# Inverse square roots by exponential and logarithm instead of square root and reciprocal, in a fused six-layer transformer kernel

## The reference

```python
# first stack, 4 layers: mixers diff, moba, swa, diff
for i in range(4):
    h = h + mixer_i(rms_norm(h, attn_norm_g[i]))
    h = h + square(relu(rms_norm(h, mlp_norm_g[i]) @ w_up[i])) @ w_down[i]
h = rms_norm(h, final_norm_g)

# second stack, 2 layers
def layer(x):
    proj = rms_norm(x, norm_g) @ w_in            # 3104 columns, cut into ten parts
    y_conv = pointwise(silu(layer_norm(conv31(a * sigmoid(a_glu))))) * silu(z_conv)
    y_mla  = attention(rms_norm(c_q) @ w_uq, rms_norm(c_kv) @ w_ukv, ...) * silu(z_mla)
    y_sg   = (sg_w @ layer_norm(gelu(v)) + sg_b) * gelu(u) * silu(z_sg)
    return x + concat(rms_norm(y_conv), rms_norm(y_mla), rms_norm(y_sg)) @ w_out

def rms_norm(x, g): return x * rsqrt(mean(x * x) + 1e-6) * g
```

## Time and profile before

| | |
|---|---|
| median of three runs | 1731.67 us (1728.75 to 1737.34) |
| profiled execution | 1732.1 us, span 1730.4 us |
| TensorE busy | 1560.4 us, 90% of the span |
| VectorE busy | 961.6 us, 56% |
| ScalarE busy | 802.0 us, 46% |
| GpSimd busy | 165.6 us, 10% |
| mean granted clock of TensorE | 0.947 of full speed |

### The profile page before, as it was taken

The page is one execution under the profiler, slowest core; times in us unless marked ns, Lnnn a source line. Parts: engine busy times, 40 slices in busy tenths (PEclk is TensorE's granted clock), DMA queues, the critical chain, the costliest instruction groups (busy, mean ns, idle before and its releaser), DMA issues. The chain is left out here.

```text
span 1730.4 us, 21899 instructions
## 1 busy us (share of the span) xinstructions
PE 1560.4 (90%) x9045; PEld 1343.7 (78%) x9045; DVE 961.6 (56%) x1177; ACT 802.0 (46%) x1170; POOL 165.6 (10%) x165
## 2 busy tenths in 40 slices
PE   7978999999889999888999998889999787698778
PEld 5756899987679998666999886669998676587666
DVE  4554545465555455654555555445555386668754
ACT  5346543354344334433444454454444454565463
POOL 2000000000000000000000000000000295009700
PEclk8998999999999999998999999889999898899878
DMA  8312455543225554321554551224555422253220
GB/s 296 107 49 98 147 195 194 189 155 143 92 104 195 195 181 158 123 98 49 189 180 179 183 205 49 98 98 170 180 185 193 142 89 89 80 184 121 92 97 25
DMA packets 100615, 241.96 MB, mean 140 GB/s; under 512 B 2642, under 2 KB 11644, under 8 KB 100540
## 3 DMA queue, kind: packets, MB, share of 16 engines
q1 hardware_dynamic: 98848, 237.25, 38.6%
q0 software_dynamic: 1344, 3.52, 1.0%
q10 hardware_dynamic: 348, 0.13, 0.0%
HBM read 239.84 MB, written 1.05 MB: 139 GB/s over the span
## 5 line engine op out<-in xcount | busy, mean ns | idle before, releaser
L1233 DVE TENSOR_TENSOR wlo<-raw,whi 128x2048 fp32r<-128x2048 f32 (+3 forms) x240 | 509.2, 2158 | 237.6 <-ACT whi L501 237.4
L501 ACT ACTIVATE whi<-raw 128x2048 fp32r<-128x2048 f32 (+3 forms) x240 | 418.8, 1790 | 170.6 <-PE pair L862 168.6
L860 PE MATMUL pair<-whi,xhi 128*128 128x512 f32 (+2 forms) x752 | 316.2, 421 | 53.7 <-DVE wlo L1233 38.6
L861 PE MATMUL pair<-wlo,xhi 128*128 128x512 f32 (+2 forms) x752 | 302.8, 403 | 0.0
L862 PE MATMUL pair<-whi,xlo 128*128 128x512 f32 (+2 forms) x752 | 301.4, 401 | 0.0
L860 PE MATMUL pair<-xhi,whi 128*128 128x256 f32 x1024 | 291.2, 284 | 7.0 <-DVE xlo L1262 7.0
L862 PE MATMUL pair<-xhi,wlo 128*128 128x256 f32 x1024 | 290.0, 283 | 0.0
L861 PE MATMUL pair<-xlo,whi 128*128 128x256 f32 x1024 | 290.0, 283 | 0.0
L860 PEld LDWEIGHTS pair<-whi,xhi 128*128 128x128 f32 x752 | 153.1, 204 | 91.3 <-DVE wlo L1233 43.1
L860 PEld LDWEIGHTS pair<-xhi,whi 128*128 128x128 f32 x1024 | 196.5, 192 | 10.4 <-issue 6.9
L860 PE MATMUL pair<-whi,ahi 128*128 128x512 f32 x512 | 200.0, 391 | 0.0
(11 more groups left out here) (235 smaller groups left out, 1707.3 us busy)
## 6 DMA issues: line engine op xcount, KB each, us to landing
raw<-in_mlp_w_up SPq DMA_DIRECT2D x32, 2048.0 KB, 8.4
raw<-in_mlp_w_down SPq DMA_DIRECT2D x32, 2048.0 KB, 7.7
raw<-in_diff_w_in SPq DMA_DIRECT2D x11, 2048.0 KB, 7.9
raw<-in_w_in SPq DMA_DIRECT2D x10, 2048.0 KB, 7.8
raw<-in_moba_w_in SPq DMA_DIRECT2D x6, 2048.0 KB, 7.8
raw<-in_diff_w_out SPq DMA_DIRECT2D x4, 2048.0 KB, 7.8
raw<-in_w_uq SPq DMA_DIRECT2D x4, 1152.0 KB, 5.5
raw<-in_moba_w_out SPq DMA_DIRECT2D x2, 2048.0 KB, 7.8
```

What stands on the lines that cost most here:

```text
L501: act.activation(whi[:, s, cols], raw[:, s, cols], ACT.Copy).then_inc(*t["hi_split"].one())
L860: pe.matmul(dst, x_hi, w_hi, start=first, stop=False)
L861: pe.matmul(dst, x_hi, w_lo, start=False, stop=False)
L1233: dve.tensor_tensor(wlo[:, s, cols], raw[:, s, cols], whi[:, s, cols].bitcast(FP32), ALU.subtract)\
```

## The change

The factor is computed as exp(-0.5 * ln(mean + 1e-6)) on ScalarE, and one Newton step on VectorE refines it: with guess y and x = mean + 1e-6, the factor is y * (1.5 - 0.5 * x * y * y), four instructions each of which waits for the one before (`refined`). ScalarE's logarithm reads the sum of squares itself, with the division as its scale and 1e-6 as its bias, a column `eps` that GpSimd fills at the start. So ScalarE no longer waits for VectorE's `var`, which is computed beside it. In a layer norm the logarithm reads the variance.

Logarithm and exponential are in one set, and this set is also loaded by name (`preload_act_table_set`) behind each sigmoid, gelu, sine and gate silu, where attention's exponentials then find it too. ScalarE's list had 45 table loads, all outside of the loops, and has 19 now: three at the start and eight in each layer of the second stack (ahead of and behind sigmoid, ahead of and behind gelu, ahead of the silu in `conv_norm`, behind `gates` 0, ahead of and behind `gates` 1). 29 square roots become 29 exponentials and 33 logarithms; 29 reciprocals become 116 small instructions on VectorE.

The diff, cut to its core. The functions that make the factor, on ScalarE:

```diff
                     act.activation(junk[n % len(junk)][:, 0:src.shape[-1]], src, ACT.Square, accum_out=ss[:, at + n:at + n + 1])\
                         .then_inc(*t["squares_summed"].one())
 
-            def roots(n, at=0):
+            def inverse_roots(dst, log, parts):
+
+                for (at, n, w), src in parts:
+                    m = act.activation(log[:, at:at + n], src, ACT.Ln, scale=1.0 / w, bias=eps[:, 0:1])
+                m.then_inc(*t["log_taken"].one())
+                act.wait_ge(*t["log_taken"].now())
+                some = slice(parts[0][0][0], at + n)
+                return act.activation(dst[:, some], log[:, some], ACT.Exp, scale=-0.5)
+
+            def roots(widths, at=0):
+
+                act.wait_ge(*t["squares_summed"].now())
+                parts = []
+                for n, w in widths:
+                    parts.append(((at, n, w), ss[:, at:at + n]))
+                    at += n
+                inverse_roots(guess, lnv, parts).then_inc(*t["guess_ready"].one())
+
+            def root_of_variance():
+
                 act.wait_ge(*t["var_ready"].after())
-                act.activation(std[:, at:at + n], var[:, at:at + n], ACT.Sqrt).then_inc(*t["std_ready"].one())
+                inverse_roots(guess, lnv, [((6, TT, 1), bn2[:, :, 1])]).then_inc(*t["guess_ready"].one())
 
             def norm(g, root=True, fresh=False, waiting=1, launch=False):
...
                     elif what == "split":
                         split((n,))
 
-            def roots16(n, at=0):
-                act.wait_ge(*t["sum16_ready"].after())
-                act.activation(std16[:, at:at + n], ss16[:, at:at + n], ACT.Sqrt).then_inc(*t["std16_ready"].one())
+            def roots16(n, w, at=0):
+
+                inverse_roots(guess16, lnv16, [((at, n, w), ss16[:, at:at + n])]).then_inc(*t["guess16_ready"].one())
 
             def mlp():
                 def up(j):
```

The places where the set is now loaded (`glu`, `gelu`, `gates`), and `prep`:

```diff
                         act.wait_ge(*t.emptied[2].now())
                         act.activation(qkv[:, :, GLU0:GLU0 + CW], qkv[:, :, GLU0:GLU0 + CW], ACT.Sigmoid)\
                             .then_inc(*t["sig_ready"].one())
+                        act.preload_act_table_set(LOG_AND_EXP)
                     elif what == "conv_in":
                         act.wait_ge(*t.filled[0].after())
                         act.activation(ypad[:, 1, CONV_K - 1:], pair[0][:, 0, SEQ:], ACT.Copy).then_inc(*t["channels_ready"].one())
...
                         x, squares = ((qbuf, flat_sm), (kfull, flat_pT))[n]
                         act.activation(squares, x[:, :, :].rearrange("p t n -> p (t n)"), ACT.Square)\
                             .then_inc(*t["heads_squared"].one())
-                        roots16(16, 16 * n)
+                        act.wait_ge(*t["sum16_ready"].after())
+                        roots16(16, QK2, 16 * n)
                     elif what == "gelu":
                         act.wait_ge(*t.emptied[2].now())
                         for c in (V0, U0):
                             act.activation(qkv[:, :, c:c + SGW], qkv[:, :, c:c + SGW], ACT.Gelu_apprx_tanh)\
                                 .then_inc(*t["gelu_ready"].one())
+                        act.preload_act_table_set(LOG_AND_EXP)
                     elif what == "conv_operand":
                         turn_split(range(2), 5, None, lhi)
                     elif what == "gates":
...
                         act.wait_ge(*t.emptied[2].now())
                         for c, w in ((ZS0, SGW),) if n else ((ZC0, CW), (ZM0, MLAW)):
                             act.activation(qkv[:, :, c:c + w], qkv[:, :, c:c + w], ACT.Silu).then_inc(*t["zsilu_ready"].one())
+                        act.preload_act_table_set(LOG_AND_EXP)
                     elif what == "pw":
                         used()
                         t.emptied[3].n += 1
                     elif what == "v_norm":
-                        roots(TT, 6)
+                        root_of_variance()
                     elif what == "sgu_mix":
                         t.filled[8].n += 1
                         t.emptied[8].n += 1
```

VectorE's side:

```diff
                         m.then_inc(*t["bank_split"].one())
                 m.then_inc(*t.emptied[p].one())
 
+            def refined(dst, x, y, factor):
+
+                chain(dve.tensor_tensor(factor, y, y, ALU.mult))
+                chain(dve.tensor_tensor(factor, factor, x, ALU.mult))
+                chain(dve.tensor_scalar(factor, factor, -0.5, 1.5, ALU.mult, ALU.add))
+                return dve.tensor_tensor(dst, factor, y, ALU.mult)
+
             def variances(widths, root=True, at=0):
 
                 some = slice(at, at + sum(n for n, _ in widths))
...
                     m = dve.tensor_scalar(var[:, at:at + n], ss[:, at:at + n], 1.0 / w, EPS, ALU.mult, ALU.add)
                     at += n
                 if root:
-                    m.then_inc(*t["var_ready"].one())
-                    dve.wait_ge(*t["std_ready"].after())
-                    dve.reciprocal(rstd[:, some], std[:, some]).then_inc(*t["rstd_ready"].one())
+                    chain(m)
+                    dve.wait_ge(*t["guess_ready"].after())
+                    refined(rstd[:, some], var[:, some], guess[:, some], fix[:, some]).then_inc(*t["rstd_ready"].one())
                     dve.wait_ge(*t["rstd_ready"].now())
                 else:
                     chain(m)
...
             def roots16(n, w, at=0):
 
                 some = slice(at, at + n)
-                dve.tensor_scalar(ss16[:, some], ss16[:, some], 1.0 / w, EPS, ALU.mult, ALU.add).then_inc(*t["sum16_ready"].one())
-                dve.wait_ge(*t["std16_ready"].after())
-                return dve.reciprocal(rstd16[:, some], std16[:, some])
+                chain(dve.tensor_scalar(var16[:, some], ss16[:, some], 1.0 / w, EPS, ALU.mult, ALU.add))
+                dve.wait_ge(*t["guess16_ready"].after())
+                return refined(rstd16[:, some], var16[:, some], guess16[:, some], fix16[:, some])
 
             def add_out(n):
...
                 chain(m)
                 for tt in range(TT):
                     m = dve.bn_aggr(bn2[:, tt, :], bn6[:, tt, :])
-                chain(m)
-                dve.tensor_scalar(var[:, 6:6 + TT], bn2[:, :, 1], EPS, None, ALU.add).then_inc(*t["var_ready"].one())
-                dve.wait_ge(*t["std_ready"].after())
-                chain(dve.reciprocal(rstd[:, 6:6 + TT], std[:, 6:6 + TT]))
+                m.then_inc(*t["var_ready"].one())
+                dve.wait_ge(*t["var_ready"].now())
+                chain(dve.tensor_scalar(var[:, 6:6 + TT], bn2[:, :, 1], EPS, None, ALU.add))
+                dve.wait_ge(*t["guess_ready"].after())
+                some = slice(6, 6 + TT)
+                chain(refined(rstd[:, some], var[:, some], guess[:, some], fix[:, some]))
                 for tt in range(TT):
                     m = dve.tensor_scalar(dst[:, tt, :], src(tt), bn2[:, tt, 0:1], rstd[:, 6 + tt:7 + tt], ALU.subtract, ALU.mult)
                 m.then_inc(*centred.one())
...
                 x = x[:, :, :].rearrange("p t (h d) -> p t h d", d=QK2)
                 squares = place[:, 0:TT * H2 * QK2].rearrange("p (t h d) -> p t h d", t=TT, d=QK2)
                 dve.wait_ge(*t["heads_squared"].after())
-                chain(dve.tensor_reduce(ss16[:, 16 * n:16 * n + 16].rearrange("p (t h) -> p t h", t=TT), squares, AXIS.X, ALU.add))
+                dve.tensor_reduce(ss16[:, 16 * n:16 * n + 16].rearrange("p (t h) -> p t h", t=TT), squares, AXIS.X, ALU.add)\
+                    .then_inc(*t["sum16_ready"].one())
+                dve.wait_ge(*t["sum16_ready"].now())
                 chain(roots16(16, QK2, 16 * n))
                 r = rstd16[:, 16 * n:16 * n + 16].rearrange("p (t h) -> p t h", t=TT).unsqueeze(3)
                 chain(dve.tensor_tensor(x, x, lanes(r, [P, TT, H2, QK2]), ALU.mult))
```

More of the change, by code:

```diff
@@ L50 @@
 QKV_COLS = {"diff": 3072, "moba": 3072, "swa": 1280}
+LOG_AND_EXP = "natural_log_exp_and_others"
 LAMBDAS = ["diff_lam_q1", "diff_lam_k1", "diff_lam_q2", "diff_lam_k2"]
@@ L179, in build @@
         var = sb("var", [P, 12])
-        std = sb("std", [P, 12])
+        lnv = sb("lnv", [P, 12])
+        guess = sb("guess", [P, 12])
+        fix = sb("fix", [P, 12])
         rstd = sb("rstd", [P, 12])
         ss16 = sb("ss16", [P, 32])
-        std16 = sb("std16", [P, 32])
+        lnv16 = sb("lnv16", [P, 32])
+        guess16 = sb("guess16", [P, 32])
+        fix16 = sb("fix16", [P, 32])
+        var16 = sb("var16", [P, 32])
         rstd16 = sb("rstd16", [P, 32])
@@ L187, in build @@
         snk = sb("snk", [P, 8, 2, 2])
+        eps = sb("eps", [P, 1])
         sums = sb("sums", [P, 8, 2, 2])
@@ L552, in norm @@
                 if root:
-                    roots(TT)
+                    roots([(TT, D)])
             def results(p, dst, w, scale):
@@ L617, in outputs @@
                     m.then_inc(*t["heads_squared"].one())
-                    roots16(4, 4 * q)
```

(7 more changed lines are left out.)

7 lines of the change are left out of this document (4 added, 3 removed).

## The result

| | before | after |
|---|---|---|
| median, us | 1730.17 (20 runs, 1720.63 to 1737.48) | 1737.86 (20 runs, 1726.09 to 1742.98) |
| ratio, 95% interval | | 1.0045 (1.0024 to 1.0065) |
| profiled execution / its span | 1732.1 / 1730.4 | 1737.35 / 1735.5 |
| granted clock in it | 0.947 | 0.948 |

The change makes the kernel 0.45% slower, inside what was called "the same" (0.5%), with an interval that lies wholly above 1. The forecast was 1736.6.

A forecast was written before the change was run, and what follows sets the result against it. TensorE, busy for 1560.4 us, was taken to bound the kernel, ScalarE paying only where TensorE waits. Terms -1.2 + 0.3 + 0.8 + 0.8 + 4.2 = +4.9 us gave 1736.6 us, range 1728 to 1744.5.

The forecast's parts named there:

- Outputs 1 and 2: Both diff layers, uncovered loads ahead of the scaled copies: factor from 1.75 to 1.45 us, 4 x -0.3 = -1.2.
- Outputs 0: Diff layers, load already covered: 0.65 us becomes 1.05; +0.3 (0 to 0.4) in the first layer, hidden in the last.
- Norm between the stacks: No load to remove there, TensorE stands for 6.96 us; the factor goes from some 0.67 to 1.45 us: +0.8.
- `gates` 0 and `prep` 1: Ahead of `llo`: a covered load moves ahead of the copies, +1.28, longer factor +0.8; +2.1 per layer, +4.2.
- Behind sigmoid, and `v_norm`: Added load's delay swallowed by a long GpSimd tap; taps end about 0.4 us later by `v_norm`'s refinement: +0.8 in all.
- All covered loads: Loads where ScalarE had to wait for VectorE anyway: removing them gives nothing back, 0.
- rival 1: ScalarE paces the kernel and every removed load pays: -24 us, about 1708; chance 0.04.
- rival 4: Port contention: refining operations beside the taps up to 0.4 us longer, taps held up too: +4, 1740.6; chance 0.08.
- Rivals 2 and 3: Clock turns worse, 1742.5 us (chance 0.16), or better, 1730.7 (chance 0.13), by 5.9 us in a second-stack layer.
- Rival 2: Longer `llo` wait lowers the first layer's clock, costing 5.9 us more: +10.8 in all, 1742.5; chance 0.16.
- the two rules: Trainium skill: about 2.66 us per table switch (sum about +2); VectorE and GpSimd lock shared ports for a whole instruction.

The follow-up runs named there:

- The two experiments on the load's place: Changed kernel with the load behind `gates` 0 moved behind the keys' square: 1734.37 us; kernel before with a square-root set load behind those silus: 1738.26 us.
- early loads with the direct factor: Changed kernel with ScalarE's exponential writing the factor itself, no refining step, loads where the change has them: 1732.33 us, ratio to before 1.0006.
- second profiles: Kernel before and changed kernel, each word for word, profiled again: 1732.99 us before, 1732.3 us after.

## Why the prediction was right

Forecast +4.9 us, measured +7.7 between the medians, +5.4 at an equal clock, 5.25 between the first profiled executions and -0.7 between the second ones. The largest term was right in its mechanism and its size; that the total came so near is luck in part. By its steps:

- *Outputs 1 and 2*: forecast 4 x -0.3; the waits went from 3.04 to 2.75, with 1.43 us for the factor where 1.45 stood. Right.
- *Outputs 0*: +0.3 forecast; between TensorE's starts at 12.07 and 129 nothing grew by more than 0.05. The slack on ScalarE took it.
- *Norm between the stacks*: +0.8; 6.96 to 7.75. Right.
- *`gates` 0 and `prep` 1*: +2.1 per layer; the waits grew by 2.16 and 2.18. The two experiments on the load's place show its parts, 1.4 and 0.75, where 1.28 and 0.8 stood. Right, and the largest term.
- *Behind sigmoid, and `v_norm`*: the step that failed. +0.4 per layer was forecast for the end of the taps, from one late refinement; the stretch grew by 1.37 and 1.49. The prediction had the taps start later, but the first long tap swallow that delay. It wasn't swallowed.
- *All covered loads*: 0; no wait in the first stack but those named here moved by it. ScalarE has 23.8 us less work and the kernel isn't faster, which ends rival 1.

What the long stretch goes with is the number of taps that are left. GpSimd starts its work in the first layer so, before, with TensorE's row at the end of the latent split:

```profile
1376.68 0.55 POOL L1872 TENSOR_SCALAR yacc<-ypad,colsA 128x256 f32<-128x256 f32 x1 [20.16 <-ACT ypad L717]
1377.33 0.93 POOL L1876 TENSOR_SCALAR tap<-ypad,colsA 128x256 f32<-128x256 f32 x1
...
1416.75 0.41 PE L860 MATMUL pair<-whi,lhi 128*128 128x384 f32 x1 [3.92 <-issue]
```

and after:

```profile
1374.30 1.66 POOL L1917 TENSOR_SCALAR yacc<-ypad,colsA 128x256 f32<-128x256 f32 x1 [21.73 <-ACT ypad L745]
1376.05 0.93 POOL L1921 TENSOR_SCALAR tap<-ypad,colsA 128x256 f32<-128x256 f32 x1
...
1413.78 0.66 PE L893 MATMUL pair<-whi,lhi 128*128 128x384 f32 x1 [3.95 <-issue]
```

The second instruction starts 39.4 us ahead of TensorE's row before, and 37.7 after. Of the 1.7 between, 1.1 is the first instruction, which starts while VectorE is in a weight split and takes 1.66 instead of 0.55 us. When TensorE's row starts, 15 of the 30 taps (a product and a sum each) aren't finished before, and 16 after; an undisturbed tap takes 1.83 us. The same holds in all 20 layers of the table: 16 taps are left in the seven with a stretch of 39.53 to 39.85, 15 in the thirteen with 36.98 to 38.38.

Two things make the taps late, the load behind sigmoid and the longer factor of `norm`. Late loads with the refinement in three operations leave 15 in both layers, early loads with the direct factor 15 in both, early loads with one operation in place of the refinement 15 in one layer and 16 in the other. Early loads with the whole refinement leave 16 in all six layers that have both. So neither of the two alone left 16 in both layers of a run. TensorE's clock has a part in it, since it moves the row that the taps are counted from. What each of the three is worth isn't separated. The contention of rival 4 comes on top, with small operations of 0.57 and 0.63 us beside taps; its share of the 1.4 isn't measured.

The terms as measured make -1.2 + 0 + 0.8 + 2.9 + 4.3 = +6.8; the first profiles differ by 5.25, the second ones by -0.7. The rest goes mostly with the clock, and in the first stack it favours the changed kernel. When TensorE turns `h` between the stacks, the changed kernel is 3.97 us ahead (8.0 in the second profiles), where the terms and a start 0.5 us earlier give about 0.9. The stretch ahead of the scaled outputs of the last diff layer shows how: 12.06 us at a clock of 0.75 before, 10.59 at 0.84 after, while the wait in it fell by 0.29. From the turning of `h` to the end the changed kernel takes 9.1 us longer (7.3 in the second profiles).

Rivals 2 and 3 both came true in the first profile, one in each layer: the first layer's MLA stretch went from 29.7 to 35.3 us, the second's from 36.1 to 29.9, so the two layers of the earlier trace rows changed places. Their prices of 5.9 were right (+5.6 and -6.2), and they cancelled. Rival 2 tied this to the longer wait for `llo`; the kernel before had both stretches behind waits of 6.49 and 6.48, so the length of that wait doesn't decide it.

In the weighing of the two rules, the row of 0.57 us in the earlier trace rows was read as agreement with what the Trainium skill, "SBUF — State Buffer", SBUF: two separate sides, says of operations that read two operands. But that row, `var`, has one tensor as its operand. After the change, beside taps, the operations that stretched were products in `latents` and `v_norm` (0.57 and 0.63) and in `prep` 0 the third operation, with one tensor (0.62), while the three products there took 0.17 to 0.18; without taps all took 0.16 to 0.18. The runs show that small operations are held up beside taps; they don't show that two operands are what it takes.

## What to carry to other kernels

In this kernel a table load cost what the engine's next idle time didn't cover: before placing one by name, look for the wait nearest ahead of its use, not for the last use of the old set. A delay that a longer piece of work seems to swallow can still come out at the end, if it leaves one more piece to do: count the pieces. When a chain of small operations replaces a load, count the steps (0.21 us each on VectorE) and the hand-overs; keeping the whole chain on one engine, with the Newton step left out and the loads late, was the only version faster than before. Where the clock moves single runs by 1%, argue from waits in the trace, and from times only over many runs with their clocks beside them.

## What was not expected of the hardware

- The granted clock of one stretch takes two values, and equal waits ahead of it don't settle which: 0.93 and 0.69 for the same 149 products behind waits of 8.66 and 8.65 us in one execution. What does settle it stays open.
- A version with shorter waits than the changed kernel's had the lower clock (0.943) and was the slowest kernel of all, 1741.12 us; another with still shorter ones had the highest, 0.955, and 1717.96. The runs of the one lie at 0.941 to 0.946, of the other at 0.953 to 0.959, so the program seems to have a say in the mean clock, though which layer gets the slow stretch changes from one execution to the next.
- Beside taps of GpSimd a product of 128x2 took 0.63 us on VectorE instead of 0.16, and one of 128x4 took 0.57. Without taps these were 0.16 to 0.17.
